# Third mixer of a two-block transformer kernel: decay rows between convolutions, slot work ahead of low parts, gates copied ahead of a split

## The reference, cut to what matters

```python
def mlstm_mixer(xn, w_in, conv_w, conv_b, ig_bias, fg_bias, head_gain, w_out):
    proj = xn @ w_in                       # 1024 q and k, 1024 v, 1024 output gate, 16 gates
    qk = silu(causal_depthwise_conv(proj[..., :1024], conv_w, conv_b))
    ig = gates[..., :8] + ig_bias
    lf = log_sigmoid(gates[..., 8:] + fg_bias)
    h = mlstm_chunkwise(q, k, v, ig, lf)   # k scaled by 64 ** -0.5
    h = h * rsqrt(mean(h * h) + 1e-6) * head_gain
    return (h * sigmoid(o_pre)) @ w_out
```

## Time and profile before

| | us |
|---|---|
| median of 3 runs | 2558.64 (2558.37 to 2558.85) |
| profiled execution, its own time | 2556.15 |
| its span in the profile | 2554.1 |
| mean granted TensorE clock in it | 0.986 of full speed |

### The profile page before, as it was taken

The page is one execution under the profiler, slowest core; times in us unless marked ns, Lnnn a source line. Parts: engine busy times, 40 slices in busy tenths (PEclk is TensorE's granted clock), DMA queues, the critical chain, the costliest instruction groups (busy, mean ns, idle before and its releaser), DMA issues.

```text
span 2554.1 us, 31166 instructions
## 1 busy us (share of the span) xinstructions
PE 2443.9 (96%) x13136; PEld 2073.4 (81%) x13136; DVE 1497.5 (59%) x2144; ACT 1018.1 (40%) x1428; POOL 73.0 (3%) x82
## 2 busy tenths in 40 slices
PE   4999999989999999999999989998999999888998
PEld 2888888857888888888888759987888899776997
DVE  5678496364778496443365555455466545575544
ACT  3312225364412224322225364344555434455443
POOL 0000001200000000000000200000000000000000
PEclk7999999999999999999999999999999999999999
DMA  7465363411556353444362615555544455433553
GB/s 277 141 185 189 127 208 106 136 50 33 165 182 198 132 192 121 149 132 148 108 222 75 144 57 185 183 179 174 181 130 151 132 182 183 152 128 101 182 182 140
DMA packets 239676, 385.83 MB, mean 151 GB/s; under 512 B 8048, under 2 KB 147440, under 8 KB 239472
## 3 DMA queue, kind: packets, MB, share of 16 engines
q1 hardware_dynamic: 236176, 372.43, 44.5%
q0 software_dynamic: 3360, 11.40, 2.1%
HBM read 382.71 MB, written 2.99 MB: 151 GB/s over the span
## 4 chain that ended last, share of the span: by engine, by line
PE 87%; DVE 6%; ACT 3%; DMA 2%; issue 1%; SPq 0%; POOL 0%; DVEq 0%; ACTq 0%
PE ps L522 27%; PE ps L524 27%; PE ps L523 27%; DVE wlo L1810 2%; ACT whi L1203 1%; PE ps L574 1%; PE ps L588 1%; DVE small L2145 1%; DMA arena<-in_w_mod 1%; DMA arena<-rpbs 1%; PE ps L824 1%; PE ps L934 0%; PE ps L960 0%; PE ps L919 0%; DVE Hlo L1963 0%
## 5 line engine op out<-in xcount | busy, mean ns | idle before, releaser
L1810 DVE TENSOR_TENSOR wlo<-raw,whi 128x2048 fp32r<-128x2048 f32 x279 | 637.2, 2284 | 640.6 <-ACT whi L1203 640.3
L1203 ACT ACTIVATE whi<-raw 128x2048 fp32r<-128x2048 f32 x279 | 532.6, 1909 | 1149.0 <-PE ps L524 860.9
L522 PE MATMUL ps<-wlo,Hhi 128*128 128x512 f32 (+1 forms) x1888 | 709.7, 376 | 23.0 <-DVE Hlo L1963 18.6
L524 PE MATMUL ps<-whi,Hhi 128*128 128x512 f32 (+1 forms) x1888 | 699.3, 370 | 0.0
L523 PE MATMUL ps<-whi,Hlo 128*128 128x512 f32 (+1 forms) x1888 | 698.8, 370 | 0.0
L522 PE MATMUL ps<-Hlo,whi 128*128 128x512 f32 (+1 forms) x1896 | 641.5, 338 | 0.0
L524 PE MATMUL ps<-Hhi,whi 128*128 128x512 f32 (+1 forms) x1896 | 638.9, 337 | 0.0
L523 PE MATMUL ps<-Hhi,wlo 128*128 128x512 f32 (+1 forms) x1896 | 638.3, 337 | 0.0
L522 PEld LDWEIGHTS ps<-wlo,Hhi 128*128 128x128 f32 x1888 | 360.2, 191 | 89.3 <-DVE Hlo L1963 20.8
L524 PEld LDWEIGHTS ps<-whi,Hhi 128*128 128x128 f32 x1888 | 359.9, 191 | 60.2
L523 PEld LDWEIGHTS ps<-whi,Hlo 128*128 128x128 f32 x1888 | 360.6, 191 | 56.7
(11 more groups left out here) (254 smaller groups left out, 1476.1 us busy)
## 6 DMA issues: line engine op xcount, KB each, us to landing
raw<-in_w_ffn_gate_up SPq DMA_DIRECT2D x88, 1024.0 KB, 5.1
raw<-in_w_mod SPq DMA_DIRECT2D x65, 1024.0 KB, 5.1
raw<-in_w_ffn_down SPq DMA_DIRECT2D x44, 1024.0 KB, 4.9
raw<-in_ffn_w_in SPq DMA_DIRECT2D x44, 1024.0 KB, 5.0
raw<-in_attn_w_in SPq DMA_DIRECT2D x36, 1024.0 KB, 5.1
raw<-in_ffn_w_out SPq DMA_DIRECT2D x22, 1024.0 KB, 4.9
raw<-in_w_in SPq DMA_DIRECT2D x16, 1024.0 KB, 5.0
raw<-in_mlstm_w_in SPq DMA_DIRECT2D x12, 1024.0 KB, 5.2
```

What stands on the lines that cost most here:

```text
L522: e.matmul(o, L[0], R[1], start=start, stop=False)
L524: return e.matmul(o, L[0], R[0], start=False, stop=stop)
L1203: e.activation(hi_of(n), slot(n), ACT.Copy).then_inc(*A.up(("hi", n)))
L1810: e.tensor_tensor(lo_of(n), slot(n), hi_of(n).bitcast(F32), ALU.subtract).then_inc(*V.up(("lo", n)))
```

## The change

There are three edits, all in the mixer `mlstm()`; TensorE's, GpSimd's and SyncE's programs stay as they are, and no operation is added or removed.

- ScalarE: the copy of the gates (line 1732) stands ahead of the `through()` that was before it.
- VectorE, rows: rows 0 and 1 are made behind the low part that follows the convolutions of j = 1; rows 2 and 3 between the convolutions of j = 2 and their low part; rows 4 and 5 likewise for j = 3; rows 6 and 7 at the start of slot 1. `slot(0)` and `slot(2)` make none.
- VectorE, slots: in `vo` the slot's work stands ahead of `through()`, for the slots with t = 1. `heads_root(1)`, until now the end of slot 11, stands behind the last `through()`.

```diff
+ROWS_AT = [(0, 1), (2, 3), (4, 5), (), (6, 7)]
...
@@ ScalarE, mlstm
                 vo(0, lambda i: None, by_unit)
-                through()
                 w.wait_ge(*T.at("gates"))
                 e.activation(GS[0:16, :], bk("gates")[0:16, 0:256], ACT.Copy).then_inc(
                     *A.up("gates", ("free", "gates")))
+                through()
                 evac(0, 0)
...
@@ VectorE, mlstm
                     for i, (u, t) in enumerate(order):
+                        slot(i)
                         if t:
                             through()
-                        slot(i)
...
                 def slot(i):
-                    if i < 3:
-                        rows_of(2 + 2 * i)
-                        rows_of(3 + 2 * i)
+                    if i < 2:
+                        for h in ROWS_AT[3 + i]:
+                            rows_of(h)
...
-                    if i == 11:
-                        heads_root(1)
...
                 for j in range(1, 4):
                     for s in range(2):
                         conv(j, s)
-                    through()
+                    if j == 1:
+                        through()
+                    for h in ROWS_AT[j - 1]:
+                        rows_of(h)
+                    if j > 1:
+                        through()
                     if j == 2:
                         w.wait_ge(*T.at("F"))
                         e.tensor_copy(Fs, bk("F")[:, 0:16].rearrange("p (t h) -> p t h", t=2)).then_inc(
                             *V.up("Fs", ("free", "F")))
-                rows_of(0)
-                rows_of(1)
                 vo(1, lambda i: slot(i), by_unit)
                 vo(2, lambda i: slot(4 + i), by_unit)
                 vo(3, lambda i: slot(8 + i), by_unit)
+                heads_root(1)
                 gated(1)
                 head_parts(1)
```

## The result

| | before | changed |
|---|---|---|
| median of 4 executions each | 2558.74 (2558.37 to 2560.36) | 2543.15 (2541.41 to 2546.8) |
| ratio, with its 95% interval | | 0.9938 [0.9923, 0.9953] |
| profiled execution, its own time | 2556.15 | 2544.04 |
| its span | 2554.1 | 2542.1 |

The change saves 15.6 by these medians, 12.0 by the spans of the two profiled executions. The forecast was 12.5 (2546.1, range 2543.5 to 2552.5): the direction held, the measured median lies 0.35 under the range. The interval of the ratio runs from 12.0 to 19.7 less, so these executions alone do not tell 12.5 from 15.6. A second set of five executions (first experiment) gave a ratio of 0.9946, 13.8 less. Lines of the changed kernel stand two or three higher: 1734 is 1732, 525 is 522, 1053 is 1050, 1083 is 1080, 1064 is 1061, 1660 is 1657, 1813 is 1810, 2405 is 2402, 2441 is 2438.

What follows compares the result with a forecast made beforehand. TensorE's queue, with its waits in the third mixer, was taken as the bound. Savings 3.5 + 5.85 + 1.45 + 0.35 + 4.0 = 15.15, less new waits 2.1 and 0.5, gave 12.5: 2558.64 to 2546.1, range 2543.5 to 2552.5.

Steps and rivals of the forecast that it cites:

- Saved: 3.5: TensorE's turn of the gates: copying them ahead of ScalarE's split removes the 3.35 wait, with 0.15 overlap.
- the new wait: TensorE at the first score product waits 2.1 for a PSUM bank held until the exponentials; bounds 0 and some 3.5.
- Decay rows: Rows made between VectorE's convolutions: TensorE's 5.85 wait for row 0 and 0.35 for row 4 go.
- the queue laid out: VectorE's new order, timed step by step: first low part at 2245.0, row 0 at 2247.3, first maxima at 2264.3.
- Slots: VectorE's slot work ahead of low parts: TensorE's three waits for turned scores at head products go, 4.0 saved.
- the slots don't pay: Rival: slot order changes nothing, rows 6 and 7 and a bank come late; 8.1 lost, 4.4 saved; chance 0.08.
- The out projection's wait: At its start TensorE waits 0.5 for the parts of the first four heads, made later; bounds 0 and 1.5.
- Saved: 1.45: First two heads' decay products: the clock's fall after the long wait for row 0 goes too.
- the new wait lowers the clock: Rival: the 2.1 wait at the first score product may bring one clock fall, 1.45 or so; 2547.6; chance 0.25.
- The median is 2.49 above the profiled execution: Whole-kernel offset of the kernel before, used to turn the profiled time into the forecast median, 2558.64 - 12.5.
- no new wait at all: Low end of the range: no wait arises for the bank or the out projection, 15.15 saved, 2543.5.
- the 15.15: Sum of savings in the mixer before new waits are taken off: 3.5 + 5.85 + 1.45 + 0.35 + 4.0.

Runs made afterwards that it cites:

- run 1: The changed kernel again, no edit, five rounds beside the kernel before: 2547.82 against 2561.43, ratio 0.9946.
- run 7: The changed kernel with the gates copied behind the split again: 2547.5 against 2560.38 for the kernel before, ratio 0.9953.
- run 2: The kernel before with only the copy of the gates moved: 2558.55 against 2561.43, ratio 0.9988.
- run 3: The kernel before with only the decay rows moved: 2558.98 against 2561.43, ratio 0.9993.
- run 6: The changed kernel with the decay rows where they were: 2553.97 against 2560.38 for the kernel before, ratio 0.9978.
- run 9: The kernel before with 23 matmuls, result overwritten, put into TensorE's wait for the first decay row: 2557.52 against 2560.64, ratio 0.9988.
- run 8: The changed kernel with the maxima of heads 0 and 1 ahead of a low part: 2546.7 against 2560.38 for the kernel before, ratio 0.9945.
- run 5: The changed kernel with VectorE's low parts ahead of the slots again: 2554.49 against 2560.38 for the kernel before, ratio 0.9978.

## Why the prediction was wrong in size and right in mechanism

- **Gates.** The wait went, but the step "Saved: 3.5" is worth 1.5 of waiting in the full change (run 7) and puts 2.2 into the next wait when it stands alone (run 2). The 2.1 of the new wait, which the prediction booked separately, is the other half of this term. The sum of the waits was right, the share was not.
- **Decay rows.** Right: no wait, and the low parts and rows within 0.6 of the queue laid out. Alone, the edit gives next to nothing (run 3); undone, it costs 8.2, of which 2.2 are the gates' (run 6). The term for the clock, 1.45, is 1.36 in run 9; the rows of the prediction give 4.03 less 2.64, 1.39.
- **The new wait** for the bank: 2.05 to 2.38, forecast 2.1, released by line 1660 (1657 before) as named. VectorE's queue stands behind it: with the maxima moved up, 1.57 of the 2.07 come back at later banks (run 8).
- **Slots.** Right: 4.0 of waits gone. The rival "the slots don't pay" put a price of 8.1 on their absence; run 5 measured 8.2, which is closer than its interval allows one to say. In its parts that rival was not exact: it had 1.9 for the bank, where run 5 has 0.74.
- **The out projection's wait**: 0.58, forecast 0.5.
- **The clock.** This is the step that failed: "Saved: 1.45", as the only fall of the clock that goes. The prediction took one fall from one profiled execution, and gave the rival "the new wait lowers the clock" 0.25, which is near what the profiles show (1 of 7). But it did not ask how often the clock falls behind the waits that go: behind the gates' wait and behind that of 2.0 the first profile had no fall, and others have. The means of four give 14.0, where the first pair gives 12.8: the clock's net term is about 2.7 (1.45 and the further 1.2; uncertain by 1.4), not 1.45, and 5.9 for a kernel before with every fall (126.08) against the changed one with none but that at its start (108.86).
- **From the profiled execution to the median.** "The median is 2.49 above the profiled execution" was carried over unchanged. The medians of the four executions lie 2.59 above the profiled one before, and 0.89 below it after (2544.04 against 2543.15): 3.5 together, which is the rest between the 12.1 of the two profiled executions' own times and 15.6. Both offsets are chance: the profiled executions of before have 2556.15, 2558.3, 2561.11 and 2555.56. So of the 3.1 by which the forecast of 12.5 missed the 15.6, some 1.2 are the clock's falls in the mixer as far as four profiles tell, and the rest is put down to which executions were taken; no run shows another cause.
- **The range.** Its low end, "no new wait at all", took in the new wait's bound, but no bound of the clock's. With the 15.15 and two more falls at 1.5, behind the gates' wait and behind that of 2.0, it would have been 2540.5 and held the result. The larger set of run 1 gives 13.8 and the mean of the mixers 14.0, both inside the range; the four executions' 15.6 is above them.

What stays open is how the clock's falls elsewhere in the program, which no edit touches, differ between executions; the spread of 7.3 in the kernel before is larger than the mixer's 4.5.

## What to carry to other kernels

Lay out the waiting engine's queue and the queues of those that it waits for, step by step with durations from the trace; the sum of a joint change can be right to half a microsecond where the single terms are not, since a wait that is removed reappears at the next thing that is late, and what one edit is worth depends on which others are there. Put work that another engine is about to need ahead of work that is needed two units later and waits itself. And before a difference of some microseconds is read from one profile of each kernel, take several: here it differed from execution to execution which waits were followed by a lower clock.

## What the runs showed of the hardware

- The same program with the same waits took 121.62 and 126.08 in the same stretch, and the changed one 108.86 and 111.88. The longer ones have the same waits within 0.4 and one or two more stretches with a granted clock of 0.5.
- Equal waits are followed by 1.2 GHz in some executions and by 2.4 GHz in others: 3.35 and 3.36 at the gates without a fall, 2.98 and 3.43 with one. The Trainium skill (TensorE: Matmul & The Clock Gate, the section on the HAM clock gate) calls the number of slow matmuls at a kernel's start run-variable, since the gate's window runs freely. These runs show such a variation behind waits in the midst of a kernel.
- Waits of 5.3 to 7.9 were followed by 1.2 GHz in 7 of 7 profiles, waits of 2.0 in 5 of 8 (head products), waits of 2.1 to 2.4 in 1 of 7 (first score product). The wait of 2.3 at the mixer's start was followed by it in 18 of 18, the nearly equal one of 2.5 for the parts of heads 4 to 7 in 6 of 16. The length of the wait alone does not settle it.
- A fall of the clock cost different amounts in different places: 3.0 behind the first score product in run 1, 1.36 at the first decay products, 0.4 where the next wait, of 0.9, took it up.
- Matmuls that compute nothing of use, put into a wait, made the kernel before faster by 3.1 (0.8 to 5.4; run 9).
